# Decay exponents of a chunked scan: the mask written once per group and bank, then only differences between heads' sums

## What is computed

```python
def step(h, inp):                      # chunks of 128 positions
    qq, kk, vv, aa = inp
    cs = jnp.cumsum(aa, axis=1)
    seg = cs[:, :, None] - cs[:, None, :]
    decay = jnp.exp(jnp.where(mask[None, :, :, None, None], seg, -jnp.inf))
    qk = jnp.einsum('bjgn,blgn->bjlg', qq, kk)
    y_intra = jnp.einsum('bjlgh,blghp->bjghp', qk[..., None] * decay, vv)
    y_inter = jnp.einsum('bjgn,bghnp->bjghp', qq, h) * jnp.exp(cs)[..., None]
    ...
y = bidir_scan(qc, kb, v_f, v_b, log_a_forward, log_a_backward)
y = y + xh * d_skip;  y = y * silu(z);  y = group_rms_norm(y) * norm_g;  out = y @ w_out
```

## Time and profile before

| | |
|---|---|
| median of 3 runs | 1761.82 us (1761.11 to 1761.87) |
| profiled execution | 1761.53 us, its span 1759.8 us |
| PE busy | 1729.4 us, 98% of the span |
| DVE busy | 1170.9 us, 67% |
| ACT busy | 790.3 us, 45% |
| POOL busy | 182.0 us, 10% |
| chain that ended last | PE 82%, DVE 12%, ACT 4%, issue 1%, DMA 1%, POOL 1% |
| TensorE's granted clock, 40 slices | 9 tenths or more of full speed in each |
| one group of the scan | about 59 us (products 1 of groups 1 and 2 are 59.1 us apart) |

### The profile page before, as it was taken

One profiled execution on the slowest core, in us unless ns is written; L12 is line 12 of the kernel. 1 busy time (PEld: TensorE's weight loads), 2 busy tenths in 40 slices (PEclk: granted clock), 3 DMA queues, 4 the chain that ended last, 5 costly groups with the idle time before them and its releaser, 6 DMA issues.

```text
span 1759.8 us, 21732 instructions
## 1 busy us (share of the span) xinstructions
PE 1729.4 (98%) x8630; PEld 1380.5 (78%) x8630; DVE 1170.9 (67%) x1653; ACT 790.3 (45%) x1364; POOL 182.0 (10%) x203
## 2 busy tenths in 40 slices
PE   9999999999999999999999999999989999999998
PEld 7887877776578888888897886777668888888887
DVE  5565774867668887663368996766684688766334
ACT  5565652642244544442244544475562445444221
POOL 0421001400000111110000000221120001111000
PEclk9999999999999999999999999999999999999999
DMA  6211123311122222233323221011112132222332
GB/s 222 96 61 59 62 96 122 95 58 60 60 72 91 93 99 100 96 91 104 92 68 114 84 99 57 25 37 37 37 49 96 48 132 96 96 96 93 99 96 72
DMA packets 44277, 147.95 MB, mean 84 GB/s; under 512 B 5264, under 2 KB 8464, under 8 KB 44048
## 3 DMA queue, kind: packets, MB, share of 16 engines
q1 hardware_dynamic: 41728, 141.89, 24.3%
q10 hardware_dynamic: 2448, 4.66, 0.9%
HBM read 144.44 MB, written 2.10 MB: 83 GB/s over the span
## 4 chain that ended last, share of the span: by engine, by line
PE 82%; DVE 12%; ACT 4%; issue 1%; DMA 1%; POOL 1%; ACTq 0%; DVEq 0%; POOLq 0%
PE bank L387 21%; PE bank L389 21%; PE bank L388 21%; DVE cv L2226 4%; DVE w_lo L349 2%; PE bank L404 2%; PE bank L406 2%; PE bank L405 2%; PE bank L2327 1%; PE bank L2288 1%; PE bank L2300 1%; PE bank L983 1%; PE bank L996 1%; DVE bank L813 1%; PE bank L2309 1%
## 5 line engine op out<-in xcount | busy, mean ns | idle before, releaser
L387 PE MATMUL bank<-a_hi,w_hi 128*128 128x512 f32 x1384 | 555.2, 401 | 2.7 <-DVE a_lo L1270 1.1
L349 DVE TENSOR_TENSOR w_lo<-raw,w_hi 128x1024 fp32r<-128x1024 f32 (+1 forms) x257 | 328.2, 1282 | 335.6 <-ACT w_hi L342 335.0
L389 PE MATMUL bank<-a_hi,w_lo 128*128 128x512 f32 x1384 | 539.3, 390 | 0.0
L388 PE MATMUL bank<-a_lo,w_hi 128*128 128x512 f32 x1384 | 539.0, 389 | 0.0
L342 ACT ACTIVATE w_hi<-raw 128x1024 fp32r<-128x1024 f32 (+1 forms) x259 | 268.1, 1042 | 307.0 <-DMA raw<-in_w_down 143.5
L387 PEld LDWEIGHTS bank<-a_hi,w_hi 128*128 128x128 f32 x1384 | 259.8, 188 | 77.1 <-issue 20.3
L388 PEld LDWEIGHTS bank<-a_lo,w_hi 128*128 128x128 f32 x1384 | 259.9, 188 | 58.9 <-issue 6.9
L389 PEld LDWEIGHTS bank<-a_hi,w_lo 128*128 128x128 f32 x1384 | 259.8, 188 | 55.1
L1357 ACT ACTIVATE u<-bank,par 128x512 f32<-128x512 f32 x88 | 68.6, 779 | 177.8 <-DVE bank L813 177.8
L387 PE MATMUL bank<-g_hi,w_hi 128*128 128x512 f32 x308 | 119.8, 389 | 0.0
L388 PE MATMUL bank<-g_lo,w_hi 128*128 128x512 f32 x308 | 119.8, 389 | 0.0
(11 more groups left out here) (398 smaller groups left out, 2543.4 us busy)
## 6 DMA issues: line engine op xcount, KB each, us to landing
raw<-in_w_up SPq DMA_DIRECT2D x88, 512.0 KB, 3.2
raw<-in_w_in SPq DMA_DIRECT2D x50, 512.0 KB, 3.2
raw<-in_w_out SPq DMA_DIRECT2D x32, 512.0 KB, 3.7
raw<-in_w_down SPq DMA_DIRECT2D x32, 512.0 KB, 3.5
raw<-in_w_xbc SPq DMA_DIRECT2D x24, 512.0 KB, 3.2
raw<-in_w_z SPq DMA_DIRECT2D x16, 512.0 KB, 3.2
raw<-in_w_down SPq DMA_DIRECT2D x16, 384.0 KB, 3.1
raw<-in_w_mem_kv SPq DMA_DIRECT2D x4, 512.0 KB, 3.2
```

Of the source, the lines that this page charges most:

```text
L349: nc.vector.tensor_tensor(w_lo[:, q % RING, 0:w], raw[:, q % RING, 0:w], w_hi[:, q % RING, 0:w].bitcast(F32), ALU.subtract).then_inc(lo_do ...
L387: nc.tensor.matmul(out, wh, rhs_hi[:, k, :], start=k == first, stop=False)
L388: nc.tensor.matmul(out, wh, rhs_lo[:, k, :], start=False, stop=False)
L389: return nc.tensor.matmul(out, wl, rhs_hi[:, k, :], start=False, stop=stop)
```

## The change

Spreads: the mask is written only by the first step of a group in each of the two banks (n < 2). The second matmul then always adds (`start=False`) onto what the bank holds, with a column of `seld` in place of `sel`: for head 0 of a group the head's own selection, for the others its selection minus that of the head before. So that a bank holds one direction, steps are counted heads first: i = n // 4, hh = n % 4 // 2, d = n % 2. Product m = 2i + d therefore takes steps 4i + d and 4i + 2 + d. `em` becomes five separate matrices, `em[n % 5]`. The spreads are issued one at a time around the products: 2 and 3 ahead of the loop, with `carried(g, 0)`; then one before and one behind products 0 to 5; `part_z` stands behind even products, `carried` of the next pair behind odd ones. `seld` is made once, on POOL, at the start of the kernel.

```diff
-    em = at("em", [P, 4, S], 56)
+    em = [at(f"em{n}", [P, S], kb) for n, kb in enumerate((56, 58, 60, 62, ST + 80))]
+    seld = at("seld", [P, 2 * SG, HPG], 103, F32R)
...
     def step_of(n):
-        return n // 4, n % 2, n % 4 // 2
+        return n // 4, n % 4 // 2, n % 2
...
-            col = SH * d + HPG * g + 2 * i + hh
-            nc.tensor.matmul(bank[4 + n % 2][:, :], ident_r[:, :], veil[:, d:d + 1, :].to_broadcast([P, TT, P]), start=True, stop=False)
-            nc.tensor.matmul(bank[4 + n % 2][:, :], sel[:, col:col + 1].to_broadcast([P, P]), cst_t[:, :], start=False, stop=True).then_inc(xp, 1)
+            if n < 2:
+                nc.tensor.matmul(bank[4 + d][:, :], ident_r[:, :], veil[:, d:d + 1, :].to_broadcast([P, TT, P]),
+                                 start=True, stop=False, skip_group_check=True)
+            nc.tensor.matmul(bank[4 + d][:, :], seld[:, SG * d + g, 2 * i + hh:2 * i + hh + 1].to_broadcast([P, P]), cst_t[:, :],
+                             start=False, stop=True, skip_group_check=True).then_inc(xp, 1)
...
-            pe.wait_ge(mlu, STEPS * g + 2 * m + 2)
+            pe.wait_ge(mlu, STEPS * g + 4 * i + 3 + d)
...
-                    n = 2 * m + hh
+                    n = 4 * i + 2 * hh + d
...
+            spread(g, 2)
+            spread(g, 3)
+            carried(g, 0)
             for m in range(8):
-                if m < 7:
-                    spread(g, 2 * m + 2)
-                    spread(g, 2 * m + 3)
-                else:
-                    if g + 1 < SG:
-                        begin(g + 1)
-                if m % 2 == 0:
-                    carried(g, m // 2)
-                if m % 2 and g + 1 < SG:
-                    part_z(4 * g + 5, m // 2)
+                i, d = m // 2, m % 2
+                if m < 6:
+                    spread(g, 4 * i + 4 + 2 * d)
+                elif d and g + 1 < SG:
+                    begin(g + 1)
                 inside(g, m)
+                if m < 6:
+                    spread(g, 4 * i + 5 + 2 * d)
+                if d == 0 and g + 1 < SG:
+                    part_z(4 * g + 5, i)
+                if d and i < 3:
+                    carried(g, i + 1)
...
-            if n >= 4:
-                act.wait_ge(intra, 8 * g + n // 2 - 1)
+            if n >= 5:
+                act.wait_ge(intra, 8 * g + 2 * ((n - 5) // 4) + (n - 5) % 2 + 1)
...
+        pool.wait_ge(sel_done, 1)
+        heads_of = sel[:, :].rearrange("p (n h) -> p n h", h=HPG)
+        nc.gpsimd.tensor_copy(seld[:, :, 0:1], heads_of[:, :, 0:1])
+        nc.gpsimd.tensor_tensor(seld[:, :, 1:HPG], heads_of[:, :, 1:HPG].bitcast(F32), heads_of[:, :, 0:HPG - 1].bitcast(F32),
+                                ALU.subtract).then_inc(sel_done, 1)
```

More of the change, by code:

```diff
@@ L2322, in inside @@
             i, d = m // 2, m % 2
-            pe.wait_ge(mlu, STEPS * g + 2 * m + 2)
+            pe.wait_ge(mlu, STEPS * g + 4 * i + 3 + d)
             for c in range(TT):
                 for hh in range(2):
-                    n = 2 * m + hh
+                    n = 4 * i + 2 * hh + d
                     mm = nc.tensor.matmul(bank[2 + i % 2][hh * HD:(hh + 1) * HD, c * P:(c + 1) * P],
-                                          xtok[:, c, (2 * i + hh) * HD:(2 * i + hh + 1) * HD], em[:, n % 4, c * P:(c + 1) * P],
+                                          xtok[:, c, (2 * i + hh) * HD:(2 * i + hh + 1) * HD], em[n % 5][:, c * P:(c + 1) * P],
                                           start=False, stop=d == 1 and c == TT - 1, skip_group_check=True)
@@ L2340, in ssd_pe @@
         pe.wait_ge(xsilu, 24)
-        pe.wait_ge(sel_done, 2)
+        pe.wait_ge(sel_done, 3)
         begin(0)
@@ L2432, in decays @@
             act.wait_ge(xp, STEPS * g + n + 1)
-            if n >= 4:
-                act.wait_ge(intra, 8 * g + n // 2 - 1)
+            if n >= 5:
+                act.wait_ge(intra, 8 * g + 2 * ((n - 5) // 4) + (n - 5) % 2 + 1)
             for c in range(TT):
-                e = nc.scalar.activation(em[:, n % 4, c * P:(c + 1) * P], bank[4 + n % 2][:, c * P:(c + 1) * P], ACT.Exp,
+                e = nc.scalar.activation(em[n % 5][:, c * P:(c + 1) * P], bank[4 + n % 2][:, c * P:(c + 1) * P], ACT.Exp,
                                          bias=lbias[:, c, d, h:h + 1])
@@ L2581, in weigh @@
                 dve.wait_ge(gl_done, g + 1)
-            nc.vector.tensor_tensor(em[:, n % 4, :], em[:, n % 4, :], gmat[:, :], ALU.mult).then_inc(mlu, 1)
+            nc.vector.tensor_tensor(em[n % 5][:, :], em[n % 5][:, :], gmat[:, :], ALU.mult).then_inc(mlu, 1)
         def evac_y(g, i):
```

## The result

The changed kernel takes 1770.83 us (median of 5 runs, 1769.98 to 1771.69) against 1761.59 us (1761.11 to 1761.87) before: ratio 1.0053, 95% interval 1.0041 to 1.0066, slower by 9.2 us. Its profiled execution took 1771.69 us, its span is 1770.0. The forecast was 1771.5.

A forecast was written before the change was run, and what follows sets the result against it. TensorE's issue was taken to bound group 0, waits for VectorE to end the loop in groups 1 and 2, VectorE most of group 3. Losses 1.2 + 3.6 + 2.65 + 2.3 = 9.8 us gave 1771.5 us, range 1762 to 1775.

The forecast's parts named there:

- What the masks are worth: All groups: 56 mask matmuls go, at most 12.9 us of TensorE's issue, won only where TensorE ends last.
- Rival D: Groups 0 to 2: TensorE never waits for the exponential, all 9.7 us of masks come off, 1752 us; chance 0.08.
- The chain behind the odd product: From product 2i - 1 to product 2i through exponential and `weigh`: 3.04 us undisturbed, so TensorE waits 0.47 us.
- GpSimd's lead: GpSimd's gate multiplication starts before `weigh` and delays it; in group 0 product 2i starts 3.84 us after product 2i - 1.
- Rival C: GpSimd doesn't hold `weigh` back: even products 3.04 us behind odd ones, about 1762 us, 1764.3 with the clock's fall; chance 0.14.
- Groups 0 to 2: Scan loops of these groups: losses of 1.2 us in group 0 and 1.8 us each in groups 1 and 2.
- Group 3: Last group: TensorE waits 5.8 us before `spread` 6, delaying product 6 by 2.65 us; the clock's fall adds 2.3 us.
- the clock's part: Group 3: the standstill lowers TensorE's clock, taken as 2.3 us, bounds 0 and 2.9 us.
- the estimate from the start of the kernel: Upper bound for the clock's fall in group 3: half of the 5.9 us slow matmul start at kernel start, 2.9 us.
- the three steps: Group 3: 18 output projection matmuls behind product 1, put at 4.3 us, to be issued after the wait for `spread` 6.
- rival A: Group 3: TensorE's clock stays up through the standstill, loss 7.5 us in all, 1769.2 us; chance 0.30.

The follow-up runs named there:

- crossed heads: Kernel before, its products of adjacent steps kept; forward steps take heads 0, 1, backward ones 1, 0, masks written once per group and bank: 1756.36 us.
- edit to `out3`: Changed kernel with the first three output projection steps of group 3 issued behind product 0 instead of product 1: 1767.35 us.
- all parts mended: Changed kernel with GpSimd's gate multiplications 0 to 2 held back, filler matmuls before product 6 in groups 1 and 2, and `out3` early: 1763.19 us.

## Why the prediction was right, step by step

**What the masks are worth.** 12.9 us was named as the most that can be won "only where TensorE is what ends last". That is so in group 0 and hardly elsewhere: they are worth 4.6 us in the new order, 4.9 in the old. Rival D had 9.7 us for groups 0 to 2, on the condition that TensorE never waits for the exponential. In the changed kernel the condition wasn't met. With crossed heads it nearly was (one wait of 0.53 us and one of 0.17 in group 0), and 2.6 + 0.9 + 0.9 = 4.4 us came in these groups: D's price was too high even there, since it left out that VectorE ends the loop in groups 1 and 2.

**The chain behind the odd product.** 3.04 us was predicted without GpSimd, 3.12 measured where GpSimd was held back (1099.10 to 1102.22); with GpSimd's lead 3.84 predicted, 3.85 measured. Shown, by taking the lead away.

**GpSimd's lead.** In after, `weigh` 6 of group 1 ends 0.55 us after GpSimd (1162.25 + 1.64 against 1161.69 + 1.65), as in the earlier trace rows. That GpSimd's start is the cause, and not a chance meeting, is shown by the run in which it starts later: 0.69 us again, in groups 0 and 1. The rule of the Trainium skill ("SBUF — State Buffer", section "Who interferes with whom") that the second to issue waits agrees with both; only that `weigh` ends 0.55 us after GpSimd and not its own 0.69 is left open by it. Rival C falls.

**Groups 0 to 2.** 1.2, 1.8 and 1.8 us predicted; 1.4, 1.8 and 1.9 measured. The 0.2 us too little in group 0 are nearly all its start: product 1 came at 1099.48, not 1099.3, and the scan had begun 0.16 us later in this execution. The steps in between hold too: less the 1.42 us that group 1 starts late, product 2 stands at 1162.53 (predicted 1162.5) and product 6 at 1176.66 (1176.7), with 1.30 us of wait before it.

**Group 3.** The standstill was put at 5.8 us and is 5.78; the loss at 2.65 + 2.3 = 4.95, and it is 10.1 - 5.1 = 5.0 us. With the clock kept up the loss of group 3 is 65.16 - 62.58 = 2.58 us (2.65 predicted), and the clock's part is 67.60 - 65.16 = 2.44 (2.3 predicted; 2.1 between the medians), which bears out the estimate from the start of the kernel. The edit to `out3` alone gave 3.5 us back. The prediction's working puts the three steps at 4.3 us and then adds 4.1; with 4.3 the sum would be 0.2 us higher, inside its range. Nor does VectorE carry "most" of group 3's chain in the kernel before: between 1262 and 1302 us it has 14.1 us of it, TensorE 12.6 and ScalarE 11.6; only from 1276 us on, where the sum uses it, it has more than half. The rule of the Trainium skill ("TensorE: Matmul & The Clock Gate", part 1) agrees, and rival A falls.

**What the steps left out.** Two things showed only when another was mended, so the sum was right without them. The clock fell also behind a wait of 2.40 us and, in some executions, behind one of 1.65. After has no wait like the first; at the second its clock stayed up in the profiled execution. Where it fell, with GpSimd held back, the last products of groups 2 and 3 stood 68.09 us apart against 67.49, so the sum would have been some 0.6 us too low there. And the remainder of 6.8 us in the new order was not split beforehand: product 0 waits for `weigh` of step 2 instead of 1, products 2 and 4 likewise for one step more, and product 6 for step 14 instead of 13. In the run with all parts mended product 7 is 2.9, 4.7 and 6.5 us behind that of the crossed heads at the end of groups 0, 1 and 2, but 1.2 us of each is the later start of the scan in that execution (1085.71 against 1084.51). That leaves 1.7, 3.5 and 5.3 us, some 1.75 a group. In group 0 0.4 of the 1.7 are there at product 0, and 1.2 are the three distances from an odd to an even product (3.12 us each against 2.58, 3.01 and 2.58). For group 3 some 1.6 of the 6.8 us remain by subtraction, an estimate. Its own profile can't say: that execution lay 2 us above the run's median, and in it the clock fell once more, so that product 4 took 1.98 us:

```profile
1290.56 1.98 PE L2330 MATMUL bank<-em,xtok 128*64 128x128 f32 x16 [1.35 <-DVE em L2594]
```

## What to carry to other kernels

Before work is taken off the engine that is busy for 98%, look stage by stage at what it waits for last: here 12.9 us of matmuls were worth 5, and an order that made every second product wait for a matrix one step later, with its places of issue, cost 14. Where an edit needs an order of the inputs (one direction per bank), look for the relabelling that gives it without moving any wait: crossing two heads did, and turned a loss of 9 us into a gain of 5. When a wait is mended and the time hardly moves, look at the granted clock and the spacing of the matmuls behind the next wait.

## What the runs showed of the hardware

- TensorE's clock fell after a wait of 2.40 us, not only after 5.78: matmuls 0.43 us apart for some 3 us behind it, and product 7 5.53 us behind product 6 where 3.94 are usual (1.6 us lost, 1.5 in group 2). Four matmuls without use in that wait kept it at 1.00. In group 3 it fell also behind waits of 1.65 and 0.23 us, in 4 us in which TensorE was busy for 0.93 + 1.20 us; of six profiled executions with the same code up to there, in three.
- A `weigh` on VectorE that came behind the start of GpSimd's multiplication ended 0.55 to 0.56 us after it and took 0.82 to 1.77 us (before) or 1.64 (after); with GpSimd held back `weigh` 6 took 0.69.
- 8 matmuls of 128x64 weights for one head take 1.01 us, and 16 for two heads in alternate column halves take 1.02 too.
- A slow clock cost nothing where VectorE set the pace: with crossed heads, 0.64 against 1.00 in one stretch of group 3 made 0.0 us.
